# Stick-breaking, pooling and cross-attention trunk with a routed expert mixer: three token blocks routed in one pass, a weight split moved, and gathered rows evacuated in two halves

## Chip, cores and metric

The kernel runs on one core of a Trainium2 chip. The metric is device time in microseconds, from the first instruction to the last with what the runtime puts around them. Engines: PE (TensorE), DVE (VectorE), ACT (ScalarE), POOL (GpSimd), SP (SyncE, here only a queue that issues DMAs). They work side by side and wait for each other by semaphores that are written out by hand.

## What is computed

One layer on x of 512 tokens by 1024 channels, in float32:

```
h = rmsnorm(x, norm_mix);  z = h @ w_in                       # q, k, v, pooling input, memory queries, gates
x = x + (sig(g0)*(stick(q,k,v)@w_up_sb) + sig(g1)*(pool(u)@w_up_pool)
         + sig(g2)*(cross(qx, mem)@w_up_x)) @ w_out
h = rmsnorm(x, norm_ffn)
gl = h @ w_group + b_group            # 4 groups: softmax, top 1
el = h @ w_router + b_router          # 16 experts: top 2 inside the chosen group, softmax of the two
x = x + sum over the two chosen experts of weight * ((silu(h@w_gate[e]) * (h@w_up[e])) @ w_down[e])
out = rmsnorm(x, norm_final)
```

## The kernel before

Tokens lie in four blocks of 128 (TB = 4, `last` = 3), the 1024 channels in eight tiles of 128 (KD = 8). Each float32 product is made of three matmuls in a faster format (`three`, L451 to L453): operands are split into a high and a low part, and the product is hi x hi, lo x hi and hi x lo. Weights come in chunks of 128 x 2048 through DMA into `raw`; ACT copies the high part into `ring_hi` (`split_hi`, L428), DVE makes the low part in `ring_lo` (`split_lo`, L434), and PE uses a chunk from a ring of three slots (`chunk`; `lo_ready` counts chunks whose low part is there, `chunk_used` those that PE has finished). Every expert takes six chunks: four for gate and up (`gate_up`), two for down (`down`). C_MOE is the number of the first expert's first chunk.

The stages are: mixer projections and attention; the merge of the three branches; the product with `w_out`, of which the first 512 columns of all blocks come first and the second 512 columns block by block (`out_block`, banks 4 to 7 of PSUM); the routing; sixteen expert tiles in a loop of seven times two, with the first two ahead of it; the final combination. Expert e works on a tile of 128 slots, and tokens are brought to slots by their rank within the expert. Slot tile 0 needs no gather: `permute` builds it on PE as a product of the normed rows h2 with 0/1 matrices `place` (one for each token block). The other tiles are gathered by GpSimd with indirect DMAs from `h2_rows`, which needs the table `x_row` (signal `rows_ready`); that table comes out of PE's `rows_of_slots` (L1381, L1382, signal `rows_ps`) and DVE's L1853 and L1854.

The routing of a block t has these steps, and they are interleaved by hand with `out_block(3)` on PE, so that PE has work while DVE decides. DVE adds the last half of the residual (`x2_half_b`, L1733); ACT squares it and takes the root; DVE ends the norm with a Newton step (`newton`) and writes h2 (L1737); PE transposes x2 (`x2_transpose`, L1304), ACT evacuates it into x2T, PE computes the 20 logits (`logits`, L1321); DVE chooses group and experts (`choose`, L1749 to L1770, sixteen dependent small operations and one more) and writes `onehot_b`; PE counts ranks (`ranks`, L1329; for block 3 also the totals, L1333); DVE copies the rank and makes `place` (`place_rows`, L1775 and L1776); PE permutes (`permute`, L1343). Block 3 differs: its x2 comes last, ACT scales its h2 (L932), GpSimd multiplies by the gain (L650), stores the rows (L652) and then clears the two gather buffers (L655).

Behind block 3 DVE makes tables of slots (L1823 to L1849), with the evacuation of slot tile 0 (`xe_lo`, L1817, after ACT's `xe_hi`, L940) in the middle, then the low part of chunk C_MOE+2, then waits for `rows_ps`, writes the row tables and the combination weights (L1853 to L1870) and makes the low part of chunk C_MOE+3. `link` makes the next DVE operation wait until the one it wraps has finished. PE, ACT and DVE work strictly in the order of the program; so does GpSimd. GpSimd also makes the constants at the start, each step behind the one before; `consts_ready` follows the last, and PE's first instruction waits for it.

## Time and profile before

| | us |
|---|---|
| median of 3 runs | 787.03 |
| lowest and highest | 786.92, 789.48 |
| profiled execution | 785.75 |
| its span | 784.0 |

Numbers of the trace are of the profiled execution; its times start at the span's start. In a row of the timeline the first number is the start, the second the duration, both in us; x8 is eight instructions merged into one row; the bracket at the end is the engine's idle time just before and what ended it. PE's matmul ends are modelled and reach a little over the start of the next one, so differences of starts are used for its pace. L451 and the like are lines of the kernel.

### The profile page before, as it was taken

The page shows a single profiled execution, that of the slowest core. Times are in us where ns is not written, and L with a number is a line of the kernel's source. Part 1 is how long each engine was busy: PE and PEld are TensorE (multiplying, and loading weights), DVE is VectorE, ACT ScalarE, POOL GpSimd, SP SyncE. Part 2 cuts the span into 40 slices and gives each one's busy share as a digit, 9 for nine tenths or more (in the row PEclk, how much of TensorE's full clock was granted, in tenths as well). Part 3 has the DMA queues.
Part 4 walks back from the last instruction along what each step waited for, and adds up shares of the span by engine and source line. Part 5 has one row for each costly group of instructions (what it writes and reads, how often), then busy time and mean ns, then how long its engine had stood idle before and what let it go on. Part 6 is the DMA issues. An engine that isn't in the chain of part 4 may idle for free.

```text
span 784.0 us, 10292 instructions
## 1 busy us (share of the span) xinstructions
PE 718.9 (92%) x3611; PEld 606.6 (77%) x3611; DVE 525.3 (67%) x567; ACT 416.9 (53%) x401; POOL 125.0 (16%) x109
## 2 busy tenths in 40 slices
PE   4999998999999999999999788999999999999820
PEld 3897977888888888888888677888888888888720
DVE  6678643466525234160756887999999999999918
ACT  7625654476332322231424336877878777877602
POOL 5000000000000000000000230333344444333120
PEclk9999997999999999999999889999999999999975
DMA  8542230000042232322593349999999999997034
GB/s 283 176 140 67 96 108 0 1 3 26 15 148 94 68 122 92 107 67 95 213 334 122 121 160 392 410 405 370 386 380 380 381 378 382 383 378 288 14 150 198
DMA packets 85313, 155.46 MB, mean 198 GB/s; under 512 B 6374, under 2 KB 37216, under 8 KB 84773
## 3 DMA queue, kind: packets, MB, share of 16 engines
q1 hardware_dynamic: 78452, 137.39, 48.5%
q0 software_dynamic: 6832, 17.69, 5.9%
q8 instruction: 18, 0.29, 0.1%
q14 instruction: 11, 0.08, 0.0%
HBM read 151.17 MB, written 12.58 MB: 209 GB/s over the span
## 4 chain that ended last, share of the span: by engine, by line
PE 86%; DVE 7%; issue 3%; ACT 2%; DMA 1%; POOLq 0%; SPq 0%; POOL 0%; DVEq 0%; ACTq 0%
PE ps L451 27%; PE ps L453 26%; PE ps L452 26%; PE ps L1393 2%; PE ps L1172 1%; PE ps L1174 1%; PE ps L1416 1%; PE ps L1343 1%; DMA y_in<-y_rows 1%; DVE x L1928 1%; DVE ring_lo L434 1%; DVE x L1935 1%; PE ps L1321 1%; ACT ring_hi L428 0%; PE ps L1087 0%
## 5 line engine op out<-in xcount | busy, mean ns | idle before, releaser
L434 DVE TENSOR_TENSOR ring_lo<-raw_a,ring_hi 128x2048 fp32r<-128x2048 f32 (+2 forms) x61 | 122.5, 2011 | 95.2 <-ACT ring_hi L428 94.8
L434 DVE TENSOR_TENSOR ring_lo<-raw,ring_hi 128x2048 fp32r<-128x2048 f32 x72 | 163.6, 2291 | 18.4 <-ACT ring_hi L428 17.9
L428 ACT ACTIVATE ring_hi<-raw 128x2048 fp32r<-128x2048 f32 x72 | 136.7, 1917 | 26.6 <-PE ps L453 25.5
L428 ACT ACTIVATE ring_hi<-raw_a 128x2048 fp32r<-128x2048 f32 (+2 forms) x61 | 103.1, 1691 | 41.8 <-PE ps L453 41.7
L451 PE MATMUL ps<-hT_hi,ring_hi 128*128 128x512 f32 x288 | 113.2, 393 | 4.3 <-DVE v_lo L1525 2.3
L453 PE MATMUL ps<-hT_hi,ring_lo 128*128 128x512 f32 x288 | 112.2, 390 | 0.0
L452 PE MATMUL ps<-hT_lo,ring_hi 128*128 128x512 f32 x288 | 112.2, 389 | 0.0
L451 PE MATMUL ps<-ring_hi,xT_hi 128*128 128x512 f32 x256 | 103.8, 406 | 5.0 <-DVE xT_lo L1817 5.0
L453 PE MATMUL ps<-ring_hi,xT_lo 128*128 128x512 f32 x256 | 101.4, 396 | 0.0
L452 PE MATMUL ps<-ring_lo,xT_hi 128*128 128x512 f32 x256 | 101.0, 394 | 0.0
L451 PEld LDWEIGHTS ps<-hT_hi,ring_hi 128*128 128x128 f32 x288 | 54.1, 188 | 16.5 <-DVE v_lo L1525 2.4
L453 PEld LDWEIGHTS ps<-hT_hi,ring_lo 128*128 128x128 f32 x288 | 54.1, 188 | 11.4
L451 PEld LDWEIGHTS ps<-ring_hi,xT_hi 128*128 128x128 f32 x256 | 48.9, 191 | 17.6 <-DVE xT_lo L1817 5.4
L452 PEld LDWEIGHTS ps<-hT_lo,ring_hi 128*128 128x128 f32 x288 | 54.1, 188 | 10.8
L453 PEld LDWEIGHTS ps<-ring_hi,xT_lo 128*128 128x128 f32 x256 | 48.7, 190 | 10.9
L452 PEld LDWEIGHTS ps<-ring_lo,xT_hi 128*128 128x128 f32 x256 | 48.9, 191 | 9.4
L451 PE MATMUL ps<-ring_hi,aT_hi 128*128 128x512 f32 x128 | 51.2, 400 | 2.7 <-DVE aT_lo L1879 2.7
L677 POOL COPY y_col<-y_row 128x1 int32 (+1 forms) x16 | 28.4, 1774 | 158.0 <-DVE ye L1884 158.0
L452 PE MATMUL ps<-ring_lo,aT_hi 128*128 128x512 f32 x128 | 49.9, 390 | 0.0
L453 PE MATMUL ps<-ring_hi,aT_lo 128*128 128x512 f32 x128 | 49.9, 390 | 0.0
L892 ACT ACTIVATE sig<-ps 128x1024 f32<-128x1024 f32 x8 | 8.2, 1029 | 69.0 <-PE ps L453 69.0
L668 POOL DMA_INDIRECT xe<-h_rows,x_col x16 | 34.4, 2152 | 13.8 <-POOL x_col L665 13.8
(318 smaller groups left out, 1282.3 us busy)
## 6 DMA issues: line engine op xcount, KB each, us to landing
raw<-in_w_down SPq DMA_DIRECT2D x25, 1024.0 KB
raw<-in_w_gate SPq DMA_DIRECT2D x47, 512.0 KB
raw<-in_w_up SPq DMA_DIRECT2D x47, 512.0 KB
raw_a<-in_w_in SPq DMA_DIRECT2D x15, 1024.0 KB
raw_a<-in_w_gate SPq DMA_DIRECT2D x17, 512.0 KB
raw_a<-in_w_up SPq DMA_DIRECT2D x17, 512.0 KB
raw_a<-in_w_down SPq DMA_DIRECT2D x7, 1024.0 KB
raw_a<-in_w_in SPq DMA_DIRECT2D x10, 512.0 KB, 7.2
```

Of the source, the lines that this page charges most:

```text
L428: act.activation(ring_hi[:, c[0] % SPLIT, 0:width], buf[:, 0:width], ACT.Copy).then_inc(hi_ready, 1)
L434: dve.tensor_tensor(ring_lo[:, s, 0:width], buf[:, 0:width], ring_hi[:, s, 0:width].bitcast(F32), ALU.subtract).then_inc(lo_ready, 1)
L451: pe.matmul(out_ap, l_hi, r_hi, start=start, stop=False, skip_group_check=True)
L452: pe.matmul(out_ap, l_hi, r_lo, start=False, stop=False, skip_group_check=True)
L453: return pe.matmul(out_ap, l_lo, r_hi, start=False, stop=stop, skip_group_check=True)
L668: pool.indirect_dma_start(xe[b][:, :], None, h2_rows[:, :], bass.IndirectOffsetOnAxis(x_col[b][:, :].bitcast(U32), 0), bounds_check=S - 1, ...
L677: pool.tensor_copy(y_col[b][:, :], y_row[:, bass.ds(tile, 1)]).then_inc(y_col_set, 1)
L892: act.activation(sig[:, i, :, :], gate_pair(i), ACT.Sigmoid).then_inc(g_sig, 1)
L1172: pe.matmul(zz[:, o:o + w], lhs[:, :], soft_hi[:, j:j + w], start=False, stop=False, skip_group_check=True)
L1174: ins = pe.matmul(zz[:, o:o + w], lhs[:, :], soft_lo[:, j:j + w], start=False, stop=jb == TB - 1, skip_group_check=True)
L1321: ins = pe.matmul(bank(LG[t])[:, o:o + NG + NE], x2T[:, t, k, :], wr[:, k, :], start=k == 0, stop=k == KD - 1)
L1393: ins = pe.transpose(bank(2, 2)[:, k * P:(k + 1) * P], xe[b][:, k * P:(k + 1) * P], ident[:, :])
```

## The change

- **Choice.** Blocks 0, 1 and 2 are chosen together (`choose_early`): three reads of the logits, then one chain of operations over all three blocks, with views that repeat `jm`, the maxima and the constants. Their ranks come from one step on PE (`ranks_early`), and `place_early` copies them at once and makes three `place_of` matrices. Block 3 keeps its own chain (`choose_last`).
- **Order on PE.** logits(2) and the first half of the transposes of block 3 stand directly behind logits(1); the eight k-steps of `out_block(3)` are cut 1, 6, 1 instead of 1, 1, 2, 2, 2; all three early ranks stand ahead of the last k-step.
- **Order on DVE.** The norm of block 2 stands ahead of all choices. The low part of chunk C_MOE+1 stands behind block 3's place and ahead of the tables. ACT scales h2 of block 3 ahead of the high part of chunk C_MOE+2.
- **Operations.** TENSOR_SCALAR becomes SCALAR_TENSOR_TENSOR with a constant tensor (`ones_f`, `three_halves`, `bigs`, three new memsets on GpSimd) in block 3's choice, in the places, in the one-column Newton step, and in the first table operation.
- **Halves.** Every tile of gathered rows is evacuated in two halves of 512 columns, by ACT and by DVE; `xe_ps`, `xe_h` and `xe_l` count two a tile. The first expert chunk waits for one half, the third for both. Slot tile 0 is built in banks 2 and 3 instead of 0 and 1, the transposes of x2 change banks with it, and the logits of block 3 move to bank 5. DVE's part for slot tile 0 stands seven operations earlier among the tables.
- **Tables.** `rows_of_slots` stands behind expert chunk 1 instead of 0.

PE ahead of the last out block, before: `x2` is block 3's transposes, `onehot_b` the ranks, `wr` the logits, `mgT_hi` out block 3, `place` the permutation.

```order
L1321 MATMUL ps<-wr,x2T 128x20 x4
L451 MATMUL ps<-ring_hi,mgT_hi 128x512
L452 MATMUL ps<-ring_lo,mgT_hi 128x512
L453 MATMUL ps<-ring_hi,mgT_lo 128x512
L451 MATMUL ps<-ring_hi,mgT_hi 128x512
L452 MATMUL ps<-ring_lo,mgT_hi 128x512
L453 MATMUL ps<-ring_hi,mgT_lo 128x512
L1343 MATMUL ps<-place,h_156 128x128 x4
L1304 MATMUL ps<-ident,x_155 128x128 x4
L1329 MATMUL ps<-onehot_b,ones_b 128x16 x2
L1329 MATMUL ps<-onehot_b,rank_tri 128x16
L1343 MATMUL ps<-place,h_156 128x128 x4
```

The same place now:

```order
L1331 MATMUL ps<-onehot_b,rank_tri 128x16
L1331 MATMUL ps<-onehot_b,ones_b 128x16 x2
L1331 MATMUL ps<-onehot_b,rank_tri 128x16
L1325 MATMUL ps<-wr,x2T 128x20 x4
L454 MATMUL ps<-ring_hi,mgT_hi 128x512
L455 MATMUL ps<-ring_lo,mgT_hi 128x512
L456 MATMUL ps<-ring_hi,mgT_lo 128x512
L1354 MATMUL ps<-place_of,h_159 128x128 x4
L1311 MATMUL ps<-ident,x_158 128x128 x4
L1354 MATMUL ps<-place_of,h_159 128x128 x4
L1325 MATMUL ps<-wr,x2T 128x20 x4
L1354 MATMUL ps<-place_of,h_159 128x128 x12
```

The ranks of block 2 stood behind the last transposes, and two k-steps of the out block behind the first half of block 3's logits; now one k-step stands there, and behind the last transposes no rank is left until block 3's.

DVE from the last early place to the last Newton step, before (`ring_lo` is the weight split, the COPY into `x2T` the evacuation of the last transposes):

```order
L1775 COPY rt_165<-ps 128x16
L1776 TENSOR_SCALAR place<-slot_no_f,rt_165,oh_84 128x128
L434 TENSOR_TENSOR ring_lo<-raw_a,ring_hi 128x2048
L1733 TENSOR_TENSOR x_155<-ps,x_155 128x512
L1795 COPY x2T<-ps 128x512
L1775 COPY rt_165<-ps 128x16
L1776 TENSOR_SCALAR place<-slot_no_f,rt_165,oh_84 128x128
L1800 SCALAR_TENSOR_TENSOR ms<-ss,ms 128x1
```

The same place now:

```order
L1832 COPY rt_168<-ps 128x48
L1827 SCALAR_TENSOR_TENSOR place_of<-slot_no_f,rt_168,oh_84 128x128 x3
L1746 TENSOR_TENSOR x_158<-ps,x_158 128x512
L1853 COPY x2T<-ps 128x512
L1857 SCALAR_TENSOR_TENSOR ms<-ss,ms 128x1
```

The split no longer stands between the early places and the last half of x2. DVE behind block 3's one-hot rows now:

```order
L1838 COPY rt_168<-ps 128x16
L1827 SCALAR_TENSOR_TENSOR place_of<-slot_no_f,rt_168,oh_84 128x128
L437 TENSOR_TENSOR ring_lo<-raw_a,ring_hi 128x2048
L1880 TENSOR_TENSOR rt_167<-rt_168,e_73 128x64
L1881 SCALAR_TENSOR_TENSOR rt_170<-ps,ones_f 128x16
L1883 SCALAR_TENSOR_TENSOR rt_170<-ps,rt_170 128x16 x2
L1884 TENSOR_TENSOR ex_before<-before,rt_170 128x256
L1886 TENSOR_REDUCE rt_171<-ex_before 128x16
L1887 SCALAR_TENSOR_TENSOR rt_172<-rt_171,base_c 128x16
L1888 SCALAR_TENSOR_TENSOR rt_166<-rt_168,rt_172 128x64
```

Here the split (L437) stands behind block 3's place, ahead of the slot tables.

```diff
+            step(pool.memset(ones_f[:, :], 1.0))
+            step(pool.memset(three_halves[:, :], 1.5))
+            step(pool.memset(bigs[:, :], BIG))
...
-            split_hi(act, K(C_MOE + 2))
             act.wait_ge(rstd3, 1)
             act.activation(h2[:, last, :], x2[:, last, :], ACT.Copy, scale=rstd[:, 11:12]).then_inc(h2_scaled, 1)
+            split_hi(act, K(C_MOE + 2))
...
-            def xe_hi(n, b=2):
-                act.wait_ge(xe_ps, n)
-                act.activation(xT_hi[:, :], bank(b, 2), ACT.Copy).then_inc(xe_h, 1)
+            def xe_hi(n):
+                for u in range(2):
+                    act.wait_ge(xe_ps, 2 * n - 1 + u)
+                    act.activation(xT_hi[:, 512 * u:512 * u + 512], bank(2 + u), ACT.Copy).then_inc(xe_h, 1)
...
-                if t == last:
-                    if k0 == 0:
-                        pe.wait_ge(place_ready, 1)
-                    else:
-                        pe.wait_ge(x2T_v, 1)
+                if t == last and k0 > 0:
+                    pe.wait_ge(x2T_v, 1)
...
+            def rank_of(t, dst):
...
+                    ins = pe.matmul(dst, (rank_tri if u == t else ones_b)[:, :], onehot_b[:, u, :], start=u == 0, stop=u == t)
+                return ins
...
+            def ranks_early():
+                pe.wait_ge(onehot_ready, last)
+                for t in range(last):
+                    ins = rank_of(t, bank(4)[:, 32 + NE * t:32 + NE * t + NE])
+                ins.then_inc(rank_ps, 1)
+
+            def ranks_last():
+                pe.wait_ge(onehot_ready, TB)
+                rank_of(last, bank(5)[:, 96:96 + NE])
+                for u in range(TB):
+                    ins = pe.matmul(bank(5)[:, 96 + NE:96 + 2 * NE], ones_b[:, :], onehot_b[:, u, :],
+                                    start=u == 0, stop=u == last)
                 ins.then_inc(rank_ps, 1)
...
-                    ins = pe.matmul(bank(0, 2)[:, k * P:(k + 1) * P], h2[:, t, k * P:(k + 1) * P], place[:, t, :],
+                    ins = pe.matmul(bank(2, 2)[:, k * P:(k + 1) * P], h2[:, t, k * P:(k + 1) * P], place_of[:, t, :],
                                     start=t == 0 and k % 4 == 0, stop=t == last, skip_group_check=True)
-                if t == last:
-                    ins.then_inc(xe_ps, 1)
+                    if t == last and k % 4 == 3:
+                        ins.then_inc(xe_ps, 1)
...
             out_block(3, 0, 1)
             logits(1)
-            ranks(0)
-            out_block(3, 1, 2)
             logits(2)
-            out_block(3, 2, 4)
             x2_transpose(3, 0, 4)
-            ranks(1)
-            out_block(3, 4, 6)
+            out_block(3, 1, 7)
+            ranks_early()
             logits(3, 0, 4)
-            out_block(3, 6, KD)
+            out_block(3, 7, KD)
             permute(0, 0, 4)
             x2_transpose(3, 4, KD)
-            ranks(2)
             permute(0, 4, KD)
             logits(3, 4, KD)
             permute(1)
             permute(2, 0, 4)
-            ranks(3)
+            ranks_last()
             permute(2, 4, KD)
             permute(3)
...
                 if read is not None:
-                    pe.wait_ge(xe_l, read)
+                    pe.wait_ge(xe_l, 2 * read)
                 for k in range(KD):
                     ins = pe.transpose(bank(2, 2)[:, k * P:(k + 1) * P], xe[b][:, k * P:(k + 1) * P], ident[:, :])
-                ins.then_inc(xe_ps, 1)
+                    if k % 4 == 3:
+                        ins.then_inc(xe_ps, 1)
 
...
+                if i == 2:
+                    pe.wait_ge(xe_l, 2 * n)
                 if i == 0:
-                    pe.wait_ge(xe_l, n)
+                    pe.wait_ge(xe_l, 2 * n - 1)
...
                 gate_up(1, C_MOE, i, None, None)
-                if i == 0:
+                if i == 1:
                     rows_of_slots()
...
+                if cols.stop - cols.start == 1:
+                    link(dve.scalar_tensor_tensor(ms[:, cols], ms[:, cols], -0.5, three_halves[:, :], ALU.mult, ALU.add))
+                else:
+                    link(dve.tensor_scalar(ms[:, cols], ms[:, cols], -0.5, 1.5, ALU.mult, ALU.add))
...
+            def choose_early():
+                for t in range(last):
+                    dve.wait_ge(lg_ps, t + 1)
+                    ins = dve.scalar_tensor_tensor(lgs[:, t, :], bank(LG[t])[:, 0:lgw], rstd[:, 8 + t:9 + t],
+                                                   bias_bc[:, :], ALU.mult, ALU.add)
+                link(ins)
+                gl, el = lgs[:, early, 0:NG], lgs[:, early, NG:lgw]
+
+                def first_max(vals, mx, n):
+
+                    link(dve.tensor_reduce(mx[:, early], vals, AX_X, ALU.max))
+                    link(dve.tensor_tensor(tmp[:, early, 0:n], vals, row(mx, n), ALU.is_equal))
+                    link(dve.tensor_tensor(tmp[:, early, 0:n], tmp[:, early, 0:n], each(jm, n), ALU.mult))
+                    link(dve.tensor_reduce(lowest[:, early], tmp[:, early, 0:n], AX_X, ALU.min))
+
+                first_max(gl, gmax, NG)
+                link(dve.tensor_tensor(gsel[:, early, 0:NG], each(jm, NG), row(lowest, NG), ALU.is_equal))
+                link(dve.scalar_tensor_tensor(gsel[:, early, 0:NG], gsel[:, early, 0:NG], BIG, each(bigs, NG),
+                                              ALU.mult, ALU.subtract))
+                link(dve.tensor_tensor(by_group(elm[:, early, :]), by_group(el),
+                                       gsel[:, early, 0:NG].unsqueeze(3).broadcast_to([P, last, NG, EPG]), ALU.add))
+                first_max(elm[:, early, :], v1, NE)
+                link(dve.tensor_tensor(m1[:, early, :], each(jm, NE), row(lowest, NE), ALU.is_equal))
+                link(dve.scalar_tensor_tensor(elm[:, early, :], m1[:, early, :], -BIG, elm[:, early, :], ALU.mult, ALU.add))
+                first_max(elm[:, early, :], v2, NE)
+                link(dve.tensor_tensor(m2[:, early, :], each(jm, NE), row(lowest, NE), ALU.is_equal))
+                dve.tensor_tensor(onehot_b[:, early, :], m1[:, early, :], m2[:, early, :], ALU.add).then_inc(onehot_ready, last)
+                link(dve.tensor_tensor(oh0[:, early].unsqueeze(2), m1[:, early, 0:1], m2[:, early, 0:1], ALU.add))
...
-                link(dve.tensor_scalar(gsel[:, t, 0:NG], jm[:, 0:NG], lowest[:, one], 1.0, ALU.is_equal, ALU.subtract))
+                link(dve.scalar_tensor_tensor(gsel[:, t, 0:NG], jm[:, 0:NG], lowest[:, one], ones_f[:, 0:NG],
+                                              ALU.is_equal, ALU.subtract))
...
-                link(dve.tensor_scalar(m2[:, t, :], jm[:, :], lowest[:, one], None, ALU.is_equal))
+                link(dve.scalar_tensor_tensor(m2[:, t, :], jm[:, :], lowest[:, one], ones_f[:, :], ALU.is_equal, ALU.mult))
...
+            def place(t):
+                dve.scalar_tensor_tensor(place_of[:, t, :], slot_no_f[:, :], rank[:, t, 0:1],
+                                         oh0[:, t:t + 1].broadcast_to([P, P]), ALU.is_equal, ALU.mult).then_inc(place_ready, 1)
+
+            def place_early():
+                dve.wait_ge(rank_ps, 1)
+                link(dve.tensor_copy(rank[:, early, :], bank(4)[:, 32:32 + NE * last].rearrange("p (t e) -> p t e", t=last)))
+                for t in range(last):
+                    place(t)
+
+            def place_last():
+                dve.wait_ge(rank_ps, 2)
+                link(dve.tensor_copy(rank[:, last, :], bank(5)[:, 96:96 + NE]))
+                place(last)
...
             x2_half_b(2)
-            choose(0)
             normed(2)
-            choose(1)
-            place_rows(0)
             dve.wait_ge(sq_a, 1)
             dve.tensor_scalar(ms[:, 6:7], ss[:, 6:7], 1.0 / D, EPS, ALU.mult, ALU.add).then_inc(ms_a, 1)
-            choose(2)
-            place_rows(1)
-            split_lo(dve, K(C_MOE + 1))
+            choose_early()
+            place_early()
             x2_half_b(3)
             dve.wait_ge(x2T_ps, TB + 1)
-            dve.tensor_copy(x2T[:, last, 4:8, :], bank(3)).then_inc(x2T_v, 1)
-            place_rows(2)
+            dve.tensor_copy(x2T[:, last, 4:8, :], bank(1)).then_inc(x2T_v, 1)
...
-            choose(3)
+            choose_last()
...
-            place_rows(3)
...
+            place_last()
+            split_lo(dve, K(C_MOE + 1))
+
+            def xe_lo(n):
+                for u in range(2):
+                    part = slice(512 * u, 512 * u + 512)
+                    dve.wait_ge(xe_h, 2 * n - 1 + u)
+                    dve.tensor_tensor(xT_lo[:, part], bank(2 + u), xT_hi[:, part].bitcast(F32), ALU.subtract).then_inc(xe_l, 1)
+
+            n_tok = bank(5)[:, 96 + NE:96 + 2 * NE]
...
-            link(dve.tensor_scalar(extra, n_tok, float(P), None, ALU.is_gt))
+            link(dve.scalar_tensor_tensor(extra, n_tok, float(P), ones_f[:, :], ALU.is_gt, ALU.mult))
...
             link(dve.scalar_tensor_tensor(past, rank, float(P), bc(base1), ALU.is_ge, ALU.mult))
+            xe_lo(1)
             link(dve.tensor_tensor(slot, slot, past, ALU.add))
...
-            xe_lo(1, 0)
...
+            dve.wait_ge(lo_ready, C_MOE + 2)
             split_lo(dve, K(C_MOE + 2))
             dve.wait_ge(rows_ps, 1)
```

## Rows read from the trace of the kernel before

**Rows 1.** The page's part 4: shares of the chain that ended last.
```profile
PE 86%; DVE 7%; issue 3%; ACT 2%; DMA 1%; POOLq 0%; SPq 0%; POOL 0%; DVEq 0%; ACTq 0%
```

**Rows 2.** Table of stages: stretch, length, busy us, clock, DMA share, GB/s.
```profile
440.00:454.00 14.00, 11.64 (x66) 11.26 (x64) 11.49 (x42) 5.34 (x6) 4.80 (x4) 0.65 0.54 188
...
490.00:740.00 250.00, 250.00 (x1182) 205.94 (x1181) 232.15 (x141) 195.63 (x141) 94.85 (x54) 1.00 0.94 355
```

**Rows 3.** Timeline of PE: start, us, line, operation, tiles; idle before.
```profile
430.39 0.18 PE L1329 MATMUL ps<-onehot_b,ones_b 128*128 128x16 bf16 x1 [1.16 <-DVE onehot_b L1769]
...
438.37 0.63 PE L1304 MATMUL ps<-ident,x 128*128 128x128 f32 x4 [3.09 <-issue]
...
448.98 0.23 PE L1329 MATMUL ps<-onehot_b,ones_b 128*128 128x16 bf16 x3 [2.10 <-DVE onehot_b L1769]
...
449.19 4.55 PE L1343 MATMUL ps<-place,h 128*128 128x128 f32 x24
456.18 0.50 PE L451 MATMUL ps<-ring_hi,xT_hi 128*128 128x512 f32 x1 [2.44 <-DVE xT_lo L1817]
...
460.63 0.19 PE L1381 MATMUL ps<-at_block,at_part 128*128 128x24 bf16 x1
...
461.05 0.47 PE L451 MATMUL ps<-ring_hi,xT_hi 128*128 128x512 f32 x1
...
469.33 1.04 PE L1393 MATMUL ps<-ident,xe 128*128 128x128 f32 x8
472.89 0.50 PE L451 MATMUL ps<-ring_hi,xT_hi 128*128 128x512 f32 x1 [2.52 <-DVE xT_lo L1817]
```

**Rows 4.** Timeline of DVE over the same stretch.
```profile
420.66 0.24 DVE L1749 SCALAR_TENSOR_TENSOR lgs<-ps,rstd,bias_bc 128x20 f32<-128x20 f32 x1 [1.00 <-PE ps L1321]
...
424.17 0.17 DVE L1769 TENSOR_TENSOR onehot_b<-picked 128x16 bf16<-128x16 f32 x1
...
435.38 2.29 DVE L434 TENSOR_TENSOR ring_lo<-raw_a,ring_hi 128x2048 fp32r<-128x2048 f32 x1
...
441.86 0.24 DVE L1749 SCALAR_TENSOR_TENSOR lgs<-ps,rstd,bias_bc 128x20 f32<-128x20 f32 x1 [0.77 <-PE ps L1321]
...
442.77 2.02 DVE L1760 TENSOR_SCALAR rt<-jm,sm 128x4 f32<-128x4 f32 x1
...
445.72 1.83 DVE L1765 TENSOR_SCALAR picked<-jm,sm 128x16 f32<-128x16 f32 x1
...
448.74 0.17 DVE L1769 TENSOR_TENSOR onehot_b<-picked 128x16 bf16<-128x16 f32 x1
...
449.84 0.22 DVE L1823 TENSOR_TENSOR rt<-rt,e 128x64 f32<-128x64 f32 x1
...
451.98 0.23 DVE L1832 TENSOR_TENSOR rt<-rt,rt 128x64 f32<-128x64 f32 x1
...
454.90 1.23 DVE L1817 TENSOR_TENSOR xT_lo<-ps,xT_hi 128x1024 fp32r<-128x1024 f32 x1 [1.50 <-ACT xT_hi L940]
...
458.18 2.28 DVE L434 TENSOR_TENSOR ring_lo<-raw_a,ring_hi 128x2048 fp32r<-128x2048 f32 x1
461.23 0.18 DVE L1853 TENSOR_SCALAR y_row<-ps 128x24 int32<-128x24 f32 x1 [0.77 <-PE ps L1382]
...
463.87 4.51 DVE L434 TENSOR_TENSOR ring_lo<-raw,ring_hi 128x2048 fp32r<-128x2048 f32 x2
```

**Rows 5.** Timeline of GpSimd (POOL) over the same stretch.
```profile
442.41 2.36 POOL L650 TENSOR_TENSOR h<-h,gffn_bc 128x1024 f32<-128x1024 f32 x1 [14.83 <-ACT h L932]
...
445.66 1.86 POOL L655 MEMSET xe<- 128x1024 f32 x2
...
464.13 2.08 POOL L665 COPY x_col<-x_row 128x1 int32<-128x1 int32 x1
```

**Rows 6.** Timeline of GpSimd at the start: two of its constants.
```profile
4.26 0.15 POOL L618 IOTA jm<- 128x16 f32 x1
4.48 0.14 POOL L620 IOTA e<- 128x16 f32 x1
```

64 lines of the change are left out of this document (26 added, 38 removed).

## Prediction, written before the changed kernel was run

> **What bounds the kernel now.** I read the chain of waits first: TensorE (PE) makes up 86% of the chain that ended last [rows 1]. The table of stages says where it is not PE: from 490 to 740 us PE is busy in all 250 us, at the full granted clock, and DVE in 232 of them; from 440 to 454 us PE has a mean granted clock of 0.65 and is not always busy [rows 2]. So whatever happens in the expert loop is hidden as long as DVE stays under PE, and whatever moves the start of the experts moves the end by as much. The timeline of PE around the routing shows the losses there [rows 3]: 1.16 us before the ranks of block 1 (430.39), 3.09 us before the last transposes (438.37), 2.10 us before the ranks of block 3 (448.98), 2.44 us before the first expert matmul (456.18) and 2.52 us before the second expert (472.89). The timeline of DVE says why [rows 4]. At 435.38 it makes the low part of weight chunk C_MOE+1 (2.29 us) while PE waits for the last half of x2. Block 3's choice takes from 441.86 to 448.91, 7.05 us; the same sixteen operations take 3.68 us for block 0 (420.66 to 424.34). The difference is two TENSOR_SCALARs of 2.02 and 1.83 us, at 442.77 and 445.72. GpSimd's rows explain them [rows 5]: its multiply runs from 442.41 to 444.77, its two memsets from 445.66 to 447.52, and each slow operation ends as GpSimd's does.
>
> **Blocks 0 to 2 jointly.** Three choices of 3.68 us become one of 22 operations: three reads of the logits and 19 dependent ones. A dependent operation of block 0 costs 3.68/16 = 0.23 us from start to start [rows 4]; the joint ones have 12 or 48 elements a partition where those had 4 or 16. The row with 64 elements (449.84) lasts 0.22 us, so I keep 0.23. Logits(2) stand two steps earlier on PE and end at about 426.4, so the choice is done at 426.6 + 19 x 0.23 = 431.0. PE, with six of the eight k-steps of out block 3 ahead of it, comes to the ranks at about 431.0: the wait of 1.16 us shrinks to 0 to 0.3. PE came free before its long wait at 438.37 - 3.09 = 435.28 [rows 3]; less 1.16, plus 0.3 and without the 0.9 of the permutation that follows, out block 3 ends at about 433.3. DVE has placed three blocks by 432.8 and is idle then, because the 2.29 us split has moved. So the last half of x2 starts at 433.3 where it started behind the split at 437.6 (435.38 + 2.2), and the last transposes start at 434.1 instead of 438.37 (-4.3).
>
> **Up to the last logits.** PE now has four transposes, eight matmuls of the permutation and eight of the logits (eight of 128x128 take 0.9 us at full clock, 1.04 with the end of the last, as at 469.33 [rows 3]), 2.2 us with DVE's copy beside them: logits end at 436.3, and DVE starts block 3's choice at 436.5 instead of 441.86 (-5.4). 1.1 us of this is the clock, which fell after the wait of 3.09 us; with no long gap ahead, I take these matmuls at full clock.
>
> **The last choice.** Unhindered it takes 3.68 us. The Newton step comes 4.7 us earlier (4.3, and block 2's placing no longer stands ahead of it), ScalarE scales h2 ahead of its weight split, and so GpSimd's multiply moves to 437.7 to 440.1, inside the choice; the memsets, 0.9 us behind it as now, to 441.0 to 442.9. The change turns every TENSOR_SCALAR here into SCALAR_TENSOR_TENSOR with a second tensor in SBUF. Does that escape GpSimd? No such operation starts inside a GpSimd operation in the trace. The nearest row is the other way round: a one-element GpSimd copy of SBUF took 2.08 us at 464.13 [rows 5], while DVE was in a TENSOR_TENSOR with two SBUF inputs (463.87) [rows 4]. So two SBUF inputs and a GpSimd operation that reads SBUF exclude each other; I take that for both directions. A memset reads nothing, and I take it as harmless. Then DVE stalls at its third such operation until 440.1, and the remaining 2.1 us end at 442.2 instead of 448.91 (-6.7). The bounds are 440.1 (nothing blocks) and 443.8 (the memsets block too: they end at 442.9 with 0.9 left).
>
> The Trainium skill ("SBUF — State Buffer", section "Who interferes with whom") speaks against the full gain: a DVE instruction with two SBUF inputs contends with a GpSimd one that reads SBUF, and not with one that only writes. By it the stall at the multiply stays and that at the memsets goes; the trace has the first half from one side only, and nothing on the second.
>
> **Behind the last choice DVE is the chain.** One us for the exponents' inputs and place(3) gives 443.2. The moved split costs 2.25 on the path here, where it had hidden nothing: 445.4. The table operations up to the evacuation took 451.98 - 449.84 = 2.1 us [rows 4]: 447.5. By then PE has permuted: ranks at 442.3, then the 24 matmuls that took 4.55 us at 449.19 with the clock partly down [rows 3]; the first half of xe is complete eight matmuls before their end, so by about 445.9, and ScalarE's half is there at 446.6. So DVE's first half starts at once, about 0.7 us (1.23 for the whole [rows 4]), and the first expert matmul starts at 448.2 instead of 456.18 (-8.0). The halves are worth about 1 us of the 2.44 us wait there.
>
> **What is given back.** The rest of the tables took 1.4 us before xT_lo and 2.1 behind it; with the second half of xe (0.6) and the split of chunk C_MOE+2 (2.28 at 458.18) DVE is at 454.8 [rows 4]. It then waits for the table matmuls, which the change puts behind expert chunk 1. Before, they started 4.45 us after the first expert matmul (460.63), at a granted clock that was low for most of it, and the next chunk at 461.05 [rows 3]. Three chunks of twelve follow by 469.33, 2.76 us each. So the tables come out at 448.2 + 4.45 + 2.76 + 0.6 = 456.0, where they came at 461.23 (-5.2). From there to the split of chunk C_MOE+3 DVE has 463.87 - 461.23 = 2.64 us of small operations, then the split, 2.29: chunk 3 can start at 461.0. PE wants it at 448.2 + 4.45 + 2.76 + 0.4 + 2.76 = 458.6, so a **new wait of about 2.4 us** appears; before, DVE had it 0.4 us ahead of need (466.6). Two more splits (4.5), the product (0.6) and half an evacuation (0.7) follow: the second expert starts at 466.9 instead of 472.89, **-6.0**. If PE's clock falls in chunk 3 after the new wait, as it did behind the waits of 2.44 and 2.52 us, that is 1.2 us later, and part of it comes back in the next chunk, where the clock fell before. I take -6.0 and -4.5 to -7.3 for this term. The gather needs rows_ready only 5 us earlier and lands before it is read.
>
> **Start and loop.** Three more memsets stand ahead of consts_ready. A step there costs 4.48 - 4.26 = 0.22 us or less [rows 6]; DVE's first copy waits for PE, which waits for these constants, and DVE then has no gap up to the first projection. So +0.55, bounds 0.3 and 0.8. The exchanged operation of the Newton step stands on the path at the start and the end, eight times; I put it at nothing, and at 8 x 0.07 = 0.5 us if it were longer by what a scalar read from a column adds (0.24 against 0.17 [rows 4]). In the loop each half evacuation adds an instruction on ScalarE and DVE, some 0.07 us a step by the fixed part of small operations, under 18 us of slack in 250 [rows 2]: 0. If it showed, 14 x 0.07 = 1 us.
>
> **Sum.** -6.0 + 0.55 = -5.5 us. The profiled execution took 785.75 us by the clock of the runs (span 784.0), the median of the runs is 787.03; I put the difference against the median: **781.5 us**.
>
> **The rivals.** (A) The forecast: the multiply blocks, the memsets don't; 0.60, 779.6 to 783.2. (B) SCALAR_TENSOR_TENSOR escapes GpSimd altogether. For it: no operation with two SBUF inputs is seen held, and the four operations from 441.86 to 442.77 took 0.91 us although the multiply had begun [rows 4, 5]. Against it: the 2.08 us copy. DVE is the chain from there to the second expert, so it gives its 2.1 us in full: 779.4, with its own spread 777.5 to 781; 0.18. (C) Both block, as they do now: +1.6, 783.1; 0.10. Here the replacement of operations does nothing and only the order pays. (D) PE's clock: if the wait for onehots (438.8 to 442.2, PE has nothing left) and the new one before chunk 3 leave it low through chunks 0 to 3, the tables come 2 to 3 us later and DVE behind them: 784; 0.07. (E) Slower: the joint choice. Its operands are views over three blocks with repeated elements. Were these 19 operations 0.8 us each instead of 0.23, ranks would come 10.8 us later, out block 3's last step behind them, and everything with it: 792. It decides from 0.52 us an operation; the 64-element row says 0.22. 0.05, with mishaps of the same sign.
>
> The range takes A, B and C with their spreads: 777.8 to 784.6. 0.5% is 3.9 us, about what a measurement of this kernel can tell from no change, so faster means below 783.1: A nearly all, B all, half of C: 0.75; within 0.20; slower 0.05.
>
> **What would show it.** **Right:** joint operations near 0.23 us; no wait over 0.5 us on PE between 426 and 436; block 3's logits read near 437.0 (with the start's 0.55); one operation of the last choice of about 2 us that ends with GpSimd's multiply, and none with the memsets; the first expert matmul near 448.8; a wait of about 2.4 us on ring_lo ahead of expert chunk 3, where before there was none; the loop's 17.8 us a step unchanged. **Wrong:** a choice without a long operation (B), with two (C), a first expert matmul after 451, or a chunk 3 that starts with no wait, in which case the gain is near 8 us and not 5.5.

## The result, and the profile after

The changed kernel takes **777.73 us** (median of 4 runs, 777.43 to 778.99); the kernel before took 787.4 beside it. The ratio is 0.9875, 95% interval 0.9854 to 0.9896: faster by 1.0 to 1.5%, where the forecast was 781.5 and its range 777.8 to 784.6. The profiled execution took 777.58 us, with a span of 775.8, against 785.75 and 784.0 before. In what follows spans are compared with spans: 8.2 us less.

PE still makes up most of the chain (the page's part 4, against [rows 1]):

```profile
PE 86%; DVE 8%; issue 2%; ACT 2%; DMA 1%; POOL 1%; POOLq 0%; DVEq 0%; ACTq 0%
```

The stretch from 440 to 454 us [rows 2] has a mean granted clock of 0.88 where it had 0.65 (the last figures of the row are clock, DMA share, GB/s):

```profile
440.00:454.00 14.00, 9.78 (x65) 8.94 (x64) 12.96 (x41) 6.28 (x7) 4.80 (x4) 0.88 0.75 243
```

The timeline of PE after, to be held against [rows 3]; a wide matmul of the three-term product starts 0.23 us after the last at 2.4 GHz and 0.43 after it at 1.2 GHz, and its modelled length is then 0.39 or 0.63:

```profile
424.47 3.64 PE L1325 MATMUL ps<-wr,x2T 128*128 128x20 f32 x32
...
430.00 0.63 PE L455 MATMUL ps<-ring_lo,mgT_hi 128*128 128x512 f32 x1
...
445.34 0.23 PE L1331 MATMUL ps<-onehot_b,ones_b 128*128 128x16 bf16 x3 [3.04 <-DVE onehot_b L1823]
...
445.56 4.55 PE L1354 MATMUL ps<-place_of,h 128*128 128x128 f32 x24
451.29 0.50 PE L454 MATMUL ps<-ring_hi,xT_hi 128*128 128x512 f32 x1 [1.19 <-DVE xT_lo L1874]
...
457.77 0.47 PE L454 MATMUL ps<-ring_hi,xT_hi 128*128 128x512 f32 x1 [0.34 <-DVE ring_lo L437]
...
462.50 0.50 PE L454 MATMUL ps<-ring_hi,xT_hi 128*128 128x512 f32 x1 [1.73 <-DVE ring_lo L437]
...
465.38 1.03 PE L1400 MATMUL ps<-ident,xe 128*128 128x128 f32 x8
468.10 0.50 PE L454 MATMUL ps<-ring_hi,xT_hi 128*128 128x512 f32 x1 [1.69 <-DVE xT_lo L1874]
```

The timeline of DVE after, against [rows 4]:

```profile
420.50 0.69 DVE L1746 TENSOR_TENSOR x<-ps,x 128x512 f32<-128x512 f32 x1 [1.90 <-PE ps L456]
...
428.15 0.24 DVE L1772 SCALAR_TENSOR_TENSOR lgs<-ps,rstd,bias_bc 128x20 f32<-128x20 f32 x1 [1.55 <-PE ps L1325]
...
430.12 0.21 DVE L1780 TENSOR_TENSOR rt<-rt,sm 128x48 f32<-128x48 f32 x1
...
432.60 0.21 DVE L1795 TENSOR_TENSOR onehot_b<-picked 128x48 bf16<-128x48 f32 x1
...
434.58 0.21 DVE L1832 COPY rt<-ps 128x48 f32<-128x48 f32 x1 [1.69 <-PE ps L1331]
...
436.20 0.69 DVE L1746 TENSOR_TENSOR x<-ps,x 128x512 f32<-128x512 f32 x1 [0.50 <-PE ps L456]
...
439.57 0.24 DVE L1802 SCALAR_TENSOR_TENSOR lgs<-ps,rstd,bias_bc 128x20 f32<-128x20 f32 x1 [0.32 <-PE ps L1325]
...
440.74 2.22 DVE L1815 SCALAR_TENSOR_TENSOR rt<-rt,lgs 128x16 f32<-128x16 f32 x1
...
445.11 0.17 DVE L1823 TENSOR_TENSOR onehot_b<-picked 128x16 bf16<-128x16 f32 x1
...
446.21 2.28 DVE L437 TENSOR_TENSOR ring_lo<-raw_a,ring_hi 128x2048 fp32r<-128x2048 f32 x1
...
457.55 0.17 DVE L1911 TENSOR_SCALAR y_row<-ps 128x24 int32<-128x24 f32 x1
...
460.16 6.70 DVE L437 TENSOR_TENSOR ring_lo<-raw,ring_hi 128x2048 fp32r<-128x2048 f32 x3
```

And GpSimd, against [rows 5]:

```profile
440.58 2.36 POOL L656 TENSOR_TENSOR h<-h,gffn_bc 128x1024 f32<-128x1024 f32 x1 [14.82 <-ACT h L937]
...
443.82 1.86 POOL L661 MEMSET xe<- 128x1024 f32 x2
```

What the reader is to see: one choice for three blocks, 428.15 to 432.9, with 0.21 us an operation; one long operation in the last choice, 440.74, that ends with GpSimd's multiply (442.94), and none beside its memsets; no wait of PE over 0.5 us up to 442; a new wait of 1.73 us on ring_lo ahead of the fourth chunk (462.50); and the second expert at 468.10 instead of 472.89. The surprise comes behind it. The next lines are the transposes of act_e (the first, and the fifteenth, 14 steps later) of before, and then the same two of after:

```profile
480.11 0.60 PE L1416 MATMUL ps<-ident,act_e 128*128 128x128 f32 x4
...
729.21 0.60 PE L1416 MATMUL ps<-ident,act_e 128*128 128x128 f32 x4
```

```profile
473.68 0.60 PE L1426 MATMUL ps<-ident,act_e 128*128 128x128 f32 x4
...
721.39 0.60 PE L1426 MATMUL ps<-ident,act_e 128*128 128x128 f32 x4
```

The second expert starts 4.79 us earlier, its transposes 6.43 earlier, and 14 steps later it is 7.82. The step of the loop fell from 17.793 to 17.694 us.

**One table carries the rest.** The span of every profile is cut at three rows: the last wait for the out block of token block 2 (the subtraction into x ahead of the routing, 418.97 in before, 420.50 in after), the first transposes of act_e, and the fifteenth. "Start" is up to the first, "routing" from the first to the second, "step" a 14th of what lies up to the third, "tail" the rest. Median and profiled time are of the runs, the other columns of the profiled execution.

```
kernel        median  profiled  start   routing  step    tail
before        787.4   785.75    418.97  61.14    17.793  54.79
after         777.73  777.58    420.50  53.18    17.694  54.41
a_full        786.67  783.45    420.26  57.64    17.780  54.88
a_ts          780.34  780.08    419.82  56.33    17.694  54.43
a_gain        776.34  778.80    420.49  53.72    17.734  54.62
a_split       779.78  779.78    421.13  53.17    17.693  56.00
a_full_fill   780.49  782.13    420.49  54.32    17.797  56.43
b_fill        784.46  784.20    419.59  59.09    17.782  54.77
b_half        782.87  782.96    420.84  57.92    17.707  54.54
b_rest        781.72  779.95    419.41  54.36    17.734  56.16
a_fill        780.22  780.22    419.81  54.78    17.694  56.20
a_gain_fill   777.36  777.04    419.71  51.18    17.733  56.15
best1         776.64  776.83    419.63  51.53    17.694  56.22
best2         777.08  777.02    419.56  51.75    17.694  56.18
best3         776.36  776.63    421.20  51.45    17.693  54.55
a_tail        777.36  776.89    419.63  53.25    17.694  54.51
```

"Start" lies anywhere from 419.56 to 421.20 in twelve kernels whose code is the same there, and "tail" either at 54.4 to 54.9 or at 56.0 to 56.4. The rows tell where such a difference arises: against before's, after's rows of DVE stand 0.04 us earlier at 198 us and 1.51 later at 211, and from 190 to 200 us after has a granted clock of 0.83 where before has 1.00; the longer tails have matmuls at half clock behind the wait ahead of the last down projection. So it is the clock's doing and no part's price, and it is why a single median that moves by 2 us proves little here.

### The profile page after: what moved, and what is told of

The parts are those of the page before. It is cut to its first block, busy times and chain, and to the rows that moved or that the text cites. A ratio compares the mean times of both kernels' runs of the same rounds, so it can differ in the third digit from the quotient of the medians.

```text
span 775.8 us, 10306 instructions
## 1 busy us (share of the span) xinstructions
PE 713.5 (92%) x3611; PEld 603.8 (78%) x3611; DVE 518.9 (67%) x554; ACT 417.8 (54%) x418; POOL 123.9 (16%) x112
## 3 DMA queue, kind: packets, MB, share of 16 engines
q0 software_dynamic: 6832, 17.69, 6.0%
## 4 chain that ended last, share of the span: by engine, by line
PE 86%; DVE 8%; issue 2%; ACT 2%; DMA 1%; POOL 1%; POOLq 0%; DVEq 0%; ACTq 0%
PE ps L454 26%; PE ps L456 26%; PE ps L455 26%; PE ps L1400 2%; DVE ring_lo L437 1%; PE ps L1179 1%; PE ps L1181 1%; PE ps L1325 1%; PE ps L1426 1%; DMA y_in<-y_rows 1%; DVE x L1986 1%; DVE x L1993 1%; PE ps L1311 0%; PE ps L1094 0%; DVE soft L1650 0%
## 5 line engine op out<-in xcount | busy, mean ns | idle before, releaser
L437 DVE TENSOR_TENSOR ring_lo<-raw_a,ring_hi 128x2048 fp32r<-128x2048 f32 (+2 forms) x61 | 122.4, 2009 | 97.1 <-ACT ring_hi L431 97.1
L437 DVE TENSOR_TENSOR ring_lo<-raw,ring_hi 128x2048 fp32r<-128x2048 f32 x72 | 163.3, 2291 | 11.7 <-ACT ring_hi L431 9.6
L431 ACT ACTIVATE ring_hi<-raw 128x2048 fp32r<-128x2048 f32 x72 | 138.3, 1921 | 25.3 <-PE ps L456 25.3
L454 PE MATMUL ps<-ring_hi,xT_hi 128*128 128x512 f32 x256 | 101.4, 396 | 4.9 <-DVE xT_lo L1874 2.9
```

Of the source, the lines that this page charges most:

```text
L431: act.activation(ring_hi[:, c[0] % SPLIT, 0:width], buf[:, 0:width], ACT.Copy).then_inc(hi_ready, 1)
L437: dve.tensor_tensor(ring_lo[:, s, 0:width], buf[:, 0:width], ring_hi[:, s, 0:width].bitcast(F32), ALU.subtract).then_inc(lo_ready, 1)
L454: pe.matmul(out_ap, l_hi, r_hi, start=start, stop=False, skip_group_check=True)
```

## Experiments

**a_full: the halves undone.** Everything else as in the changed kernel.

```diff
-                for u in range(2):
-                    act.wait_ge(xe_ps, 2 * n - 1 + u)
-                    act.activation(xT_hi[:, 512 * u:512 * u + 512], bank(2 + u), ACT.Copy).then_inc(xe_h, 1)
+                act.wait_ge(xe_ps, n)
+                act.activation(xT_hi[:, :], bank(2, 2), ACT.Copy).then_inc(xe_h, 1)
...
-                if i == 2:
-                    pe.wait_ge(xe_l, 2 * n)
-                if i == 0:
-                    pe.wait_ge(xe_l, 2 * n - 1)
+                if i == 0:
+                    pe.wait_ge(xe_l, n)
```

> The changed kernel with one part undone: the gathered rows are evacuated whole again, one copy of 1024 columns on ScalarE and one subtraction on VectorE, for every expert. Theory H (the halves are worth something in the loop too, where the step from expert to expert fell from 17.79 to 17.69 us): the loop's step is 17.79 again (+1.4 over 14 steps), and the first and the second expert start later by the half that they no longer skip, about 1.2 us once each on VectorE's chain; second expert at 469.3, span 778.4, time 780.2. Rival R (the shorter step has another cause, the halves are hidden there): the step stays 17.69, second expert 469.3, time 778.8. Rival N (the first wait is set by something else): second expert within 0.3 of 468.1.

Measured: 786.67 us (781.44 to 788.58, 11 runs), ratio to before 0.9985 (0.9964 to 1.0006). Without the halves the median gain is gone. The timeline of PE:

```profile
453.26 0.50 PE L454 MATMUL ps<-ring_hi,xT_hi 128*128 128x512 f32 x1 [2.44 <-DVE xT_lo L1868]
...
455.13 0.63 PE L455 MATMUL ps<-ring_lo,xT_hi 128*128 128x512 f32 x1
...
466.02 0.50 PE L454 MATMUL ps<-ring_hi,xT_hi 128*128 128x512 f32 x1 [2.16 <-DVE ring_lo L437]
...
472.31 0.50 PE L454 MATMUL ps<-ring_hi,xT_hi 128*128 128x512 f32 x1 [2.38 <-DVE xT_lo L1868]
...
477.90 0.60 PE L1422 MATMUL ps<-ident,act_e 128*128 128x128 f32 x4
...
726.82 0.60 PE L1422 MATMUL ps<-ident,act_e 128*128 128x128 f32 x4
```

The step is 17.78 again, as theory H says (1.2 us over 14 steps). The rest is larger than any theory had it. The wait ahead of the first expert is 2.44 us instead of 1.19, and eight wide matmuls behind it (454.75 to 458.12) run at half the clock, which they did not in after. Even so the profiled execution, 783.45, is one of the quicker of this kernel's runs, which spread over 7 us. The spread goes with the clock: the four executions up to 783.45 had a mean granted clock of 0.966 to 0.970 over the span, the seven from 786.05 on 0.959 to 0.962.

**a_full_fill: is it the clock?** The same kernel with transposes of ident into an unread bank, ahead of the last ranks (20), the first expert (18), its fourth chunk (14) and the second expert (18); they compute nothing that is used.

```diff
+            def fill(n):
+                for _ in range(n):
+                    pe.transpose(bank(7)[:, 0:P], ident[:, :], ident[:, :])
+
+            fill(20)
             ranks_last()
...
+            fill(18)
             for i in range(4):
+                if i == 3:
+                    fill(14)
                 gate_up(1, C_MOE, i, None, None)
```

> The kernel of a_full (whole evacuation of the gathered rows) with transposes of the identity into a bank that nobody reads, put into TensorE's waits: 20 ahead of the last ranks, 18 ahead of the first expert, 14 ahead of its fourth chunk, 18 ahead of the second expert. They compute nothing that is used. Theory C (a_full stands at 786.7 and not at the 780.2 that was expected because TensorE's clock falls after its waits of 2.2 to 3 us): no matmul at half clock from 446 to 500, the second expert at 469.9 instead of 472.3, and the median near 781 with a narrow spread. Rival W (the waits themselves are the loss): the median stays above 785.

Measured: 780.49 us (779.52 to 782.13), ratio 0.9918 (0.9888 to 0.9948). 6.2 us less than a_full by the medians (5.3 by the ratios), with no work taken away and 70 transposes added. The table of stages from 440 to 452 for a_full and for a_full_fill, and the latter's first and second expert in the timeline of PE:

```profile
440.00:452.00 12.00, 7.77 (x51) 7.29 (x49) 9.58 (x29) 5.88 (x6) 4.80 (x4) 0.72 0.68 223
```

```profile
440.00:452.00 12.00, 9.75 (x92) 9.27 (x91) 11.13 (x32) 6.11 (x6) 4.81 (x4) 1.00 0.68 225
```

```profile
451.84 0.50 PE L454 MATMUL ps<-ring_hi,xT_hi 128*128 128x512 f32 x1 [1.39 <-DVE xT_lo L1877]
...
469.26 0.50 PE L454 MATMUL ps<-ring_hi,xT_hi 128*128 128x512 f32 x1 [0.41 <-DVE xT_lo L1877]
```

The granted clock is 1.00 where it was 0.72, the second expert starts at 469.26 (expected 469.9), and the spread shrinks from 7.1 to 2.6 us. The routing of the two profiles differs by 3.3 us; the rest of the 6.2 goes with a_full's slow executions, while no execution of a_full_fill had a mean clock under 0.967. Theory C holds.

**b_fill: the same in the kernel before**, 18 transposes ahead of each of the first two experts, no other edit (the same function, called in two places).

> The kernel before with 18 such transposes ahead of the first expert and 18 ahead of the second, nothing else. Theory C: the stretches at half clock behind the two waits go (456.8 to 460 costs 1.7, 474 to 477 costs 1.6 in the profile of before), the median falls by 2.4 to 3.5, to 784. Rival W: 786.9, within 0.5. Rival F (the transposes themselves run at half clock and outlast the wait): 788.

Measured: 784.46 us (783.59 to 786.52), ratio 0.9971 (0.9953 to 0.9989). Routing falls by 2.05 us, 1.64 of it behind the second expert. So 2 to 3 us of before's median (2.3 by the ratio, 3.0 by the medians beside it) were the clock behind its own two waits of 2.44 and 2.52 us [rows 3].

**b_half: the halves alone in the kernel before**, from the second expert on (the first waits for both).

```diff
-                if i == 0:
-                    pe.wait_ge(xe_l, n)
+                if before is not None and i == 2:
+                    pe.wait_ge(xe_l, 2 * n)
+                if i == 0:
+                    pe.wait_ge(xe_l, 2 * n - 1 if before is not None else 2)
```

> The kernel before with the evacuation by halves alone, from the second expert on (the first waits for both halves, since its rows lie in banks 0 and 1 here, into which the first chunk is added up). Theory H+C (the halves shorten the loop's step by 0.1 and the second expert's wait by 1.2, and with the shorter wait the clock stays up behind it): 1.4 + 1.2 + 1.6 = 4.2 less, 782.7. Rival H (no part by the clock): 784.3. Rival R (the loop's step is not theirs): 785.7 or more.

Measured: 782.87 us (780.85 to 785.78), ratio 0.9949 (0.9927 to 0.9971). The row that decides is PE's second expert, where before waited 2.52 us and then ran seven matmuls at half clock. The fences are b_half's second expert, the first of before's seven, and the table of stages over 472 to 480 for b_half and for before:

```profile
473.18 0.50 PE L451 MATMUL ps<-ring_hi,xT_hi 128*128 128x512 f32 x1 [1.67 <-DVE xT_lo L1823]
```

```profile
474.03 0.63 PE L452 MATMUL ps<-ring_lo,xT_hi 128*128 128x512 f32 x1
```

```profile
472.00:480.00 8.00, 6.82 (x32) 5.67 (x33) 5.77 (x5) 4.57 (x5) 1.06 (x1) 1.00 0.95 343
```

```profile
472.00:480.00 8.00, 7.11 (x24) 5.68 (x25) 3.59 (x3) 3.14 (x2) 1.05 (x1) 0.79 1.01 364
```

A wait of 1.67 us, and a clock of 1.00 instead of 0.79 behind it. Routing is 3.2 us shorter (2.8 expected) and the step 17.707. Theory H+C holds for the step and for the clock (1.64 us from the second expert to the transposes). The wait shrank by 0.85 where 1.2 was expected; the half itself is 0.54 on DVE (0.73 us from the start of its subtraction to the second expert, 1.27 in before). The other 1.0 us of routing arose earlier: the tables' first row came 2.85 us behind the first expert's start instead of 4.45, since the clock stood behind a wait of 1.41 us there. And it is one profile: five of the twelve executions, 784.57 to 785.78, had a mean clock of 0.957 to 0.959, the other seven, 780.85 to 782.96, 0.964 to 0.967.

**b_rest: the change without the joint choice, and without more.** b_half with the choice's TENSOR_SCALARs exchanged (one function chooses for every block here, so in all four) and the split behind the last places. Besides the joint choice it lacks the new order on PE, the halves for the first expert, ScalarE's earlier scaling, the exchanged operations in places and Newton step, and the new places of `rows_of_slots` and of the first `xe_lo`.

```diff
             place_rows(1)
-            split_lo(dve, K(C_MOE + 1))
...
             place_rows(3)
+            split_lo(dve, K(C_MOE + 1))
...
-                link(dve.tensor_scalar(m1[:, t, :], jm[:, :], lowest[:, one], None, ALU.is_equal))
+                link(dve.scalar_tensor_tensor(m1[:, t, :], jm[:, :], lowest[:, one], ones_f[:, :], ALU.is_equal, ALU.mult))
```

> The kernel of b_half with the last choice's three TENSOR_SCALARs as SCALAR_TENSOR_TENSOR and the second chunk's low part behind the last places: all of the change but the joint choice of three blocks (and the first expert's halves). Theory: the part that is left out is worth what the joint choice saves on VectorE ahead of the last half of x2, about 3.1 us: 781. Rival (the out block and the ranks set that time already, the joint choice is hidden): 778.

Measured: 781.72 us (779.95 to 784.14), ratio 0.9936 (0.9914 to 0.9958). By the medians what b_rest lacks is worth 4.0 us. By the profiles it is not: routing is 54.36 here and 53.18 in after, 1.2 us, and this kernel waits 2.33 us for both halves ahead of its first expert, where after waits 1.19 for one. Counted from "start", the last half of x2 begins at 16.40 us here and at 15.70 in after. So the joint choice, with the order on PE that goes with it, gave 0.7 us in these two profiles. But PE's clock had fallen in after's out block, which DVE waited for (0.50 us ahead of 436.20), while b_rest's row, at 435.81, stands right behind its places. In best3, whose code up to this row is that of the changed kernel except for what GpSimd and ScalarE do, the clock stood (start 421.20):

```profile
435.64 0.69 DVE L1760 TENSOR_TENSOR x<-ps,x 128x512 f32<-128x512 f32 x1 [0.52 <-PE ps L456]
```

That is 14.44 us after "start", 2.0 less than in b_rest. So the joint choice is worth 0.7 us at this row with the fall and 2.0 without it, between the rival (hidden by the out block and the ranks) and the 3.1 of the theory. Of the medians' other 2.8 us the step is 0.6; in b_rest six of nine executions had a mean clock of 0.961 to 0.963, where the changed kernel's four had 0.968 to 0.969. Which stretches those were no profile shows.

**a_split: the split back in front of the last half of x2.**

```diff
             place_early()
+            split_lo(dve, K(C_MOE + 1))
             x2_half_b(3)
...
             place_last()
-            split_lo(dve, K(C_MOE + 1))
```

> The changed kernel with the second weight chunk's low part back ahead of the last half of x2. Theory D (VectorE's chain sets the last choice, and the low part lies in a wait where it stands now): the last half of x2 starts 2.3 later, the one-hot and the first expert too, the second expert by 1.5 to 2.3 (VectorE has 2.3 less to do behind the first expert's start): time 779.5. Rival P (the chain behind the first expert's start is VectorE's and only the sum of its work counts): first expert +2.3, third chunk and second expert within 0.4: 777.8.

Measured: 779.78 us (778.82 to 781.64), ratio 0.9911 (0.9894 to 0.9927). The number is that of theory D, 779.5, but of the 2.2 us between the profiles 0.63 are in "start" and 1.6 in the tail, both far from the edit: routing is 53.17 against 53.18. That isn't rival P either, for the first expert is not 2.3 us later: counted from "start" it comes at 30.30, and in after at 30.79. The clock stood up through out block 3 in this profile (none of the slow matmuls that after has from 428.35), so the ranks came 1.3 us sooner after "start", and the split (434.96, 2.29 us) cost the one-hot 0.3 us and no more. From the one-hot to the first expert it is 0.8 us less than in after, where the split stands in that stretch. So moving the split is worth nothing in these two profiles, and about 1.3 by estimate had the clock fallen here too (the 1.3 us that the ranks came sooner). It isn't measured better than that: against best3, where the clock stood too, the last half of x2 is 1.6 us later here (16.03 and 14.44 after "start"), and part of that is given back behind the one-hot.

**a_ts: the last choice's TENSOR_SCALARs back.** The same exchange as in b_rest, the other way.

> The changed kernel with the last choice's three SCALAR_TENSOR_TENSOR rows written as TENSOR_SCALAR again, with the same result. Theory L (a TENSOR_SCALAR waits while GpSimd clears its buffers, a form with two SBUF inputs doesn't): one row of the last choice is 1.5 to 1.9 us long and ends with the MEMSET of GpSimd; the last one-hot, the first and the second expert come 1.6 later: time 779.2. It may gain what the row at 440.74 loses now to GpSimd's multiplication (2.2 us) if a TENSOR_SCALAR passes beside that: then the sum is -0.4, 777.2. Rival: neither operation is sensitive to the clearing: 777.6, no long row but the one beside the multiplication.

Measured: 780.34 us (779.08 to 781.99), ratio 0.9918 (0.9902 to 0.9934). Timeline of DVE, then of GpSimd:

```profile
440.03 2.23 DVE L1814 SCALAR_TENSOR_TENSOR rt<-rt,lgs 128x16 f32<-128x16 f32 x1
...
442.97 2.04 DVE L1818 TENSOR_SCALAR picked<-jm,sm 128x16 f32<-128x16 f32 x1
```

```profile
439.86 2.37 POOL L656 TENSOR_TENSOR h<-h,gffn_bc 128x1024 f32<-128x1024 f32 x1 [14.78 <-ACT h L937]
...
443.12 1.86 POOL L661 MEMSET xe<- 128x1024 f32 x2
```

The operation with two SBUF inputs is held by the multiply, to 442.26 (the multiply ends at 442.23). The TENSOR_SCALAR at 442.97, 0.23 us elsewhere, lasts 2.04 and ends at 445.01; the memsets end at 444.98. In after the SCALAR_TENSOR_TENSORs at 443.95 and 444.84, beside the memsets, took 0.17 and 0.23 us. The one-hot comes 1.77 us later after "start" (1.6 expected), routing is 3.2 longer: behind the longer wait for ranks (4.85 us) PE's clock was low in the permutation and again from 465.4 to 469.6.

**a_gain: the multiply ahead of the last choice.**

```diff
-                    pool.wait_ge(h2_scaled, 1)
-                    pool.tensor_tensor(h2[:, t, :], h2[:, t, :], gffn_bc[:, :], ALU.mult).then_inc(h2_ready, 1)
+                    pool.wait_ge(x2_half, t + 1)
+                    pool.tensor_tensor(h2[:, t, 0:512], x2[:, t, 0:512], gffn_bc[:, 0:512], ALU.mult).then_inc(h2_scaled, 1)
+                    pool.wait_ge(x2_ready, t + 1)
+                    pool.tensor_tensor(h2[:, t, 512:1024], x2[:, t, 512:1024], gffn_bc[:, 512:1024], ALU.mult).then_inc(h2_scaled, 1)
...
-            act.activation(h2[:, last, :], x2[:, last, :], ACT.Copy, scale=rstd[:, 11:12]).then_inc(h2_scaled, 1)
+            act.wait_ge(h2_scaled, 2)
+            act.activation(h2[:, last, :], h2[:, last, :], ACT.Copy, scale=rstd[:, 11:12]).then_inc(h2_ready, 1)
```

> The changed kernel with GpSimd's multiplication of the last token block by the gain made in two halves ahead of ScalarE's scaling, as soon as each half of x2 is there, instead of behind it; the same products in another order. No GpSimd operation that reads SBUF is then left beside the last choice. Theory L (the row at 440.74 is 2.2 us long because of that multiplication): the last one-hot at 443.1 instead of 445.1, first expert 449.3, second expert 466.1, time 775.6. Rival W (another wait takes its place: the rows of the last block reach memory no earlier, or the tables and the low part of the weights set the third chunk): second expert at 467.5 or later, 777. Rival S (the multiplication now holds up the second half of x2 or the copy behind it by 1 us each): 777.6.

Measured: 776.34 us (776.14 to 778.80), ratio 0.9863 (0.9848 to 0.9879). The profiled execution is the 778.80, and shows both what the edit gives and what takes it:

```profile
443.04 0.17 DVE L1827 TENSOR_TENSOR onehot_b<-picked 128x16 bf16<-128x16 f32 x1
```

```profile
449.23 0.80 PE L454 MATMUL ps<-ring_hi,xT_hi 128*128 128x512 f32 x1 [2.82 <-DVE xT_lo L1878]
449.82 0.63 PE L455 MATMUL ps<-ring_lo,xT_hi 128*128 128x512 f32 x1
...
461.96 0.50 PE L454 MATMUL ps<-ring_hi,xT_hi 128*128 128x512 f32 x1 [2.18 <-DVE ring_lo L437]
...
468.59 0.50 PE L454 MATMUL ps<-ring_hi,xT_hi 128*128 128x512 f32 x1 [1.14 <-DVE xT_lo L1878]
```

The operation of 2.22 us is gone (0.18 at 440.72), and the one-hot stands at 443.04 as expected (443.1). But PE then waits 2.82 us ahead of the first expert and 2.18 ahead of the fourth chunk, with seven and eight matmuls at half clock behind them, and the second expert is 0.5 us later than in after. The other three executions, 776.14 to 776.41, are 2.4 us quicker, with a mean clock of 0.969 where the profiled one has 0.965: as if without one or both.

**Filling the waits of the quicker kernels.** a_fill and a_gain_fill are after and a_gain with such transposes; best1 adds the move of DVE's rows for the overflow table and the weights; best2 also puts a step of the out block between the routing matmuls of blocks 1 and 2; best3 is best1, and a_tail is after, with 16 transposes ahead of the last down projection.

```diff
+            split_lo(dve, K(C_MOE + 3))
+            split_lo(dve, K(C_MOE + 4))
+            link(dve.tensor_tensor(incl, obase, extra, ALU.add))
...
+            dve.tensor_copy(tab[:, :], rt[13][:, 0, 0:8]).then_inc(route_ready, 1)
             gated(1)
             xe_lo(2)
+            split_lo(dve, K(C_MOE + 5))
```

> The changed kernel with unused transposes in TensorE's waits: 20 ahead of the last ranks, 8 each ahead of the first expert, its fourth chunk and the second expert. Theory C: its profile has one stretch at half clock here that can be filled, the permutation behind the last ranks (24 in 4.55 us against 2.92), and it is only partly on the path, since VectorE has the low part and the tables to make meanwhile: 0.3 to 1.0 less than the changed kernel, 777.0. Rival: what remains is VectorE's chain, 777.7.

> The kernel of a_gain with unused transposes in TensorE's waits: 6 ahead of the last ranks, 20 ahead of the first expert, 14 ahead of its fourth chunk, 6 ahead of the second expert. Theory C: the two stretches at half clock of a_gain's profile (449.2 to 452.6 and 462.8 to 466.3) go, second expert at 466.2, 775.6 or a little less than a_gain's median of 776.3, profile included. Rival: no different from a_gain's median, since its other executions had no such stretch: 776.3.

> As a_gain_fill (8 transposes ahead of the fourth chunk), and VectorE's six rows for the table of overflow tiles and five for the weights moved behind the low parts that the fourth chunk and the second expert wait for. Theory D (the fourth chunk and the second expert wait for VectorE's chain): the fourth chunk waits 2.1 less, and the second expert is then bound by the gathered rows, which land at about 463: second expert at 465.2, 1.0 less than a_gain_fill, 774.6. Rival G (the gather already sets the second expert): the same time as a_gain_fill.

> As best1, and one step of the last out block put between the routing matmuls of block 1 and of block 2. Theory C: TensorE's clock fell at 428.4 in the changed kernel behind 32 routing matmuls of 20 columns in a row; with 3 wide matmuls between them it stays up, the out block ends 1.6 earlier less 0.7 for the joint choice that starts later: 0.9 less than best1, 773.7. Rival: the clock falls all the same, 0 to +0.7: 775.0.

> As best1, with 16 more unused transposes in TensorE's wait ahead of the last down projection. Theory C (best1's profile has 8 matmuls at half clock from 734.97, right behind that wait, and 1.6 us more from there to the end than the changed kernel's): they go, 775.0. Rival: the median stays 776.6, since the transposes outlast the wait or the clock falls elsewhere.

> The changed kernel with 16 unused transposes in the wait ahead of the last down projection, nothing else. Its own profile has no stretch at half clock there. Theory: no change, 777.7, from 777.2 to 777.9, and the slowest executions (779.0 of the changed kernel) may go. Rival: some of the changed kernel's unprofiled executions had such a stretch, and the median falls by up to 0.8.

Measured: a_fill 780.22 (ratio 0.9910, 0.9891 to 0.9928); a_gain_fill 777.36 (0.9868, 0.9848 to 0.9889); best1 776.64 (0.9856, 0.9835 to 0.9876); best2 777.08 (0.9860, 0.9839 to 0.9882); best3 776.36 (0.9860, 0.9832 to 0.9887); a_tail 777.36 (0.9881, 0.9854 to 0.9907).

a_fill is a miss: with the first wait filled the permutation ran at full clock (24 in 2.92 us), and so PE came to the first expert sooner and waited 1.95 us instead of 1.19; the clock fell behind that one (452.11 to 455.47, eight matmuls). That is 1.6 us more in routing; the other 1.8 are in the tail, where the clock fell too, as it did in kernels without these transposes. In a_gain_fill both stretches of a_gain are gone and routing is 51.18, 2.5 us less, but the tail took 1.5 back. best1 meets rival G:

```profile
463.44 1.09 PE L1409 MATMUL ps<-ident,xe 128*128 128x128 f32 x8 [2.00 <-DMA xe<-h_rows,x_col]
...
465.51 0.50 PE L454 MATMUL ps<-ring_hi,xT_hi 128*128 128x512 f32 x1 [0.32 <-DVE xT_lo L1887]
...
734.15 0.50 PE L454 MATMUL ps<-ring_hi,aT_hi 128*128 128x512 f32 x1 [2.42 <-DVE aT_lo L1936]
...
735.39 0.63 PE L455 MATMUL ps<-ring_lo,aT_hi 128*128 128x512 f32 x1
```

DVE's chain is out of the way, and PE waits 2.00 us for the gathered rows instead; nothing is gained over a_gain_fill up to the loop (routing 51.53 and 51.18). best2's clock fell at 428.5 as in after, so the wide matmuls in between did not keep it up in this profile. In best3 the tail's eight slow matmuls are gone (54.55 against 56.22), yet the median is only 0.3 us lower; its profile has the late "start" of 421.20, and slow transposes behind the wait for the gathered rows (463.93, 2.15 us). a_tail is 777.36 with a tail of 54.51: no change, as expected. The quickest kernels, a_gain, best3 and best1, are within 0.3 us of each other and 1.1 to 1.4 us under the changed kernel's median, and their intervals overlap with its own. a_gain is the simplest; that it beats the changed kernel was not settled.

## Why the prediction was off, step by step

The direction and the mechanism of the last choice (rival A) held; the size did not: 777.73 for 781.5, just under the range. By spans, 8.2 us went and 5.5 were forecast. Two terms that the sum had at nothing make up most of the difference: PE's clock behind the second expert's wait (1.6 us) and the loop (1.4 us). Of the prediction's own signs, the joint operations, the waits of PE up to 436 and the one long operation came as written. The first expert matmul at 451.29 met a sign of being wrong ("after 451"), block 3's logits were read at 439.57 and not near 437.0, the wait on ring_lo was 1.73 us and not 2.4, and the loop's step changed.

**Joint choice: right.** 0.20 to 0.25 us from operation to operation, 0.23 forecast; rival E has no ground.

**Out block 3 ends at 433.3: wrong by 1.4 us.** The last half of x2 started at 436.20, 2.35 us later than forecast with the constants' 0.55; 1.0 of this is the later "start", the rest is here: the clock fell to half from 428.35 to 432.07, right behind 32 small routing matmuls and four transposes, with no idle time ahead of it. DVE stood idle for 1.69 us at 434.58, waiting for ranks. Against "start" the last half of x2 comes 2.9 us earlier (4.3 forecast) and block 3's logits 3.8 (5.4 forecast). The sum had no term for the clock in this block, and its reason for full clock in the matmuls behind it, "with no long gap ahead", would not have been sufficient. Where the clock stood the forecast was right: in best3 the last half of x2 starts 14.44 us after "start", and 433.3 is 14.3 after before's.

**The last choice: right.** Held by the multiply, 2.22 us, not by the memsets. a_ts and a_gain show both halves separately. The Trainium skill ("SBUF — State Buffer", section "Who interferes with whom") had it so: two SBUF inputs contend with a GpSimd operation that reads, not with one that only writes; and it lists tensor_scalar among the forms that can take both port pairs and then contend with GpSimd. The rows agree with the first (2.22 us beside the multiply, 0.17 and 0.23 beside the memsets), and the 2.04 us of a_ts with the second in its effect; that the TENSOR_SCALAR took both port pairs no run shows.

**First expert to second expert: two errors that cancel.** The first expert came 6.4 us earlier against "start" where 8.0 were forecast, the second 6.3 where 6.0 were. The step that failed is the 4.45 us from the first expert to the tables, taken over from before: that figure held a stretch at half clock. Behind a wait of 1.19 us instead of 2.44 the clock stayed up, the tables' first row started 5.58 us after the first expert and not 7.21, and the new wait was 1.73 us and not 2.4. That the second expert came within 0.3 us of its forecast is luck.

**Clock behind the second expert's wait: left out, 1.6 us.** The prediction gave the halves their 0.6 us there and did not ask what the clock does behind a wait of 1.69 us where it had been 2.52. b_half shows the answer by itself: that edit alone, and the seven slow matmuls are gone. Behind waits of 1.67 to 1.71 us at this place none of five profiles has them (after, a_split, b_half, b_rest, a_tail). In b_fill, where transposes fill the wait, they are gone as well. Of the two profiles with a longer wait, before (2.52 us) has them and a_full (2.38) has none, so at that length the fall is not certain. This is the largest term that is missing. Rival D had looked at the clock only as a danger.

**Loop: wrong sign, 1.4 us.** "0; if it showed, 14 x 0.07 = 1 us" was for a cost. The step is 0.10 shorter, and it goes with the halves: 17.78 to 17.80 in the four kernels that evacuate whole (before, b_fill, a_full, a_full_fill), 17.69 to 17.73 in the twelve that don't. That PE was busy in all 250 us [rows 2] was read as nothing to be gained there. But busy counts modelled lengths that overlap: 0.06 us of the step lay in one start, from the first matmul of an expert to its second (563.51 to 563.80 in before; 0.23 in after). Which wait in PE's queue makes these 0.06 us, where the other 0.04 lie, and why three kernels with halves have 17.73, was not tried.

**Sum against the median: 1.1 to 1.5 us.** The difference of two profiles was put against 787.03, but before's profile lay 1.3 to 1.7 us under its medians and after's 0.15 under its own. a_full and a_full_fill show what makes such a spread: waits over 2 us behind which the clock falls in some executions and not in others.

Put together, in spans: -5.5 forecast; +1.0 start (+1.55 from the stretch with a granted clock of 0.83 from 190 to 200 us where before had 1.00, -0.5 between 114 and 135 us; the constants cost 0.4 to 0.5 as forecast), -0.3 routing, -1.6 behind the second expert, -1.4 loop, -0.4 tail: -8.2.

What stays open: why the tail had its slow stretch in seven profiles of fourteen behind the same wait of 2.4 to 2.8 us, and in which stretches b_rest's executions lost the 2.8 us that separate it from after in the medians and not in the routing.

## What to carry over

Where a wait of TensorE is followed by matmuls at half speed, price the wait at its length plus that stretch (here 2.4 to 2.5 us, plus 1.6 to 1.7 in the executions where the clock falls), and ask of every edit which such wait it shortens; b_half took 0.85 us from one wait, and 1.6 us of slow matmuls behind it went too. Take no duration from a stretch at half clock over into a forecast for a place that may run at the full one. And when medians move by 2 us, cut the profiles at rows that both kernels share before giving the difference to the edit: a_split had the expected number for a reason that had nothing to do with it.

## What the runs showed of the hardware

- TensorE's clock fell to half behind waits of 1.95, 2.15, 2.18, 2.4 to 2.8 and 3.0 us and longer in some profiles, in others not behind the same (2.4 to 2.8 ahead of the last down projection: seven falls in fourteen profiles; 2.16 and 2.38 in a_full and 2.33 in b_rest: none). Of some twenty waits of 0.9 to 1.8 us one was followed by a fall, the 1.77 of a_ts. It also fell without a wait, behind the small routing matmuls near 428, in 12 of 16 profiles. The Trainium skill ("TensorE: Matmul & The Clock Gate", section "Part 1: The HAM clock gate (the "warmup" mystery)") calls the number of slow matmuls at a kernel's start variable from run to run of one kernel. That is said of the start, which nothing here shows. The slow stretches behind the waits in the middle vary too: a_full's eleven executions spread over 7.1 us, and the longer ones have the lower mean clock.
- Transposes that nobody reads are a remedy with a price: by the medians 6.2 us gained in a_full, 3.0 in before, nothing in a_tail, and 2.5 us lost in a_fill, where a filled wait made the next one longer (1.95 us instead of 1.19) and the clock fell behind it (1.6 us in routing; the tail's share may be chance).
- A TENSOR_SCALAR of 16 columns on VectorE took 2.04 us beside a GpSimd memset and 0.23 elsewhere (a_ts); SCALAR_TENSOR_TENSOR with a second SBUF input took 0.17 to 0.23 there, and 2.22 to 2.23 beside GpSimd's multiply.
